# A transformer kernel on one core: output and down projections with the weights moving, layer norms along the free axis

## The chip, the cores and the metric

The kernel runs on one core of a Trainium2 chip. The metric is the device time of one execution in microseconds; three runs of the kernel before took 1226.73, 1228.14 and 1231.18 us, so the median is 1228.14 us. The core has TensorE (PE), which multiplies matrices into PSUM, the vector engine (DVE), the scalar engine (ACT), GpSimd (POOL) and SyncE (SP); here POOL and SP mostly issue DMAs. Work for PE is a product of a stationary operand (128x128, loaded first) and a moving one (128 rows by up to 512 columns).

## What is computed

Two transformer blocks and a third, recurrent one, on 256 tokens of 1024 features, in float32. Only the first two matter here (the recurrent block is left out below):

```python
mod = einsum('bd,ldm->lbm', silu(c), w_mod) + b_mod[:, None, :]
for i in range(2):
    sh_m, sc_m, g_m, sh_f, sc_f, g_f = split(mod[i], 6)
    h = x * (1.0 + sc_m) + sh_m
    y = even_mixer(h, ...) if i == 0 else odd_mixer(h, ...)   # both end with  o @ w_out
    x = layer_norm(ALPHA * x + (1.0 + g_m) * y, ln_mix_g[i], ln_mix_b[i])
    h = x * (1.0 + sc_f) + sh_f
    y = (silu(h @ w_gate[i]) * (h @ w_up[i])) @ w_down[i]
    x = layer_norm(ALPHA * x + (1.0 + g_f) * y, ln_ffn_g[i], ln_ffn_b[i])
```

The layer norm takes mean and variance over the 1024 features of a token. w_out is 1024x1024, w_down 2816x1024.

## The kernel before

**Layout.** Activations lie by feature: tile k of x, h and the rest holds features 128k to 128k+127 on the partitions and the 256 tokens along the free axis (272 with 16 meta tokens in the third block). A float32 product is made of three products in fp32r: every operand is split in a high and a low part, and high x high, high x low and low x high are added in PSUM (`three`, L1815 to L1821).

**Weights.** They stream in units of 128x1024 (`SEGMENTS`, L55: mod, even 20, out0 8, ffn0 44, down0 22, odd 24, out1 8, ffn1 44, down1 22, fqv 24 and on). SP loads two units at a time into `raw` (8 units), ACT makes the high part `whi` (`split`, L551), DVE the low part `wlo` (L982), each with 4 slots, three units ahead of PE (`LEAD`). A slot comes free when PE has done the unit (`units_done`). So unit m+3 is split by ACT and then DVE while PE is at unit m, and every step of `segment` on DVE is such a split and then the stage's own work.

**Stages.** In a wide segment (ffn, odd, fqv) a unit gives one output tile of 128 features: 8 input tiles x 3 products of 256 columns. The first three units of ffn0, odd, ffn1 and fqv run side by side, input tile by input tile, as h comes in (`first_units`). In out0 and out1 (`half`) and down0 and down1 (`deep`) a unit is one input tile with all eight output tiles: 8x3 products of 256 columns, whose stationary operand is a piece of the weights and whose moving operand is the activation. The sums stand in 4 banks of PSUM (two tiles a bank) or in 8.

**The layer norm** (L0 after out0, L1 after down0, L2 after out1, L3 after down1). Since features lie on the partitions, PE makes mean and variance, by products with a matrix of 1/1024:

- DVE: x = y*gate + xa, eight tiles (`residual_half` L1401, `residual_deep` L1355); xa is ALPHA*x, made earlier (`scale_x`, or DVE and ACT in odd);
- PE: eight float32 products of x, the mean (L1908, two passes each); DVE: x - mean (`subtract_mean`, L1036); ACT: squares (L586); PE: eight more, the variance (L1913); five keep-warm products whose result nobody reads (`keep_warm`, L1896); ACT: logarithm and exponential give 1/std (L589, L591);
- DVE, ACT, DVE for each tile: h as float32 (L1063), its high part (L599), its low part (L1068); then PE begins the next segment.

After L3 the RMS norm of the third block follows in the same way, without a mean (`stats(4, T2)`).

**Beside this.** DVE also makes the modulation: `side_sum(n)` (L1009) reduces a side weight of 128x1024 with silu(c), 80 in all; `SIDE_AT` says at which unit of even and out0 the first 22 stand, two more stand in `normalize(0)`, and `ffn0_sums`, the down0 segment and `ffn1_sums` hold the rest. POOL loads the side weights into a ring of five, later four slots (`load_sides`, L2410), and in odd issues the DMAs that turn pairs of q and k (`turn_pair`, L2426).

## Time and profile before

| | |
|---|---|
| median of three runs | 1228.14 us (1226.73 to 1231.18) |
| the profiled execution's own time | 1226.64 us |
| its span, first to last instruction | 1224.9 us |
| busy | PE 1170.8, DVE 883.1, ACT 613.0, POOL 61.8 us |
| granted TensorE clock, mean | 0.988 |
| DMA | 235.41 MB, 192 GB/s |

A profile comes from one execution. An engine's busy time is the time in which at least one instruction of it ran; matmuls overlap in it, since each is shown from its issue until its result is out. PEclk is the clock that was granted to TensorE, 1.00 for 2.4 GHz and 0.50 for 1.2 GHz. A row of the timeline begins with the start and the time in us; in brackets stands how long the engine was idle before it and what ended that.

### The profile page before, as it was taken

To read this page: it belongs to the slowest core of one execution; us is meant where nothing else is said; L and a number is where in the kernel's file an instruction comes from. 1 tells how busy PE (TensorE), PEld (TensorE's weight loads), DVE (VectorE), ACT (ScalarE), POOL (GpSimd) and SP (SyncE) were. 2 spreads that over 40 slices of the span, in tenths; PEclk is the share of its full clock that TensorE was granted. 3 is DMA by queue.
4 is the path that set the end of the run, shared out by engine and by line. 5 is a ranking of instruction groups with operands and counts; after the bars stand their busy time and mean duration, and the time that the engine had idled before them with its cause. 6 is when DMAs were issued, how large, how long until landed. Compare 5 with 4: busy or idle time off the path is not lost.

```text
span 1224.9 us, 24330 instructions
## 1 busy us (share of the span) xinstructions
PE 1170.8 (96%) x9394; PEld 1137.8 (93%) x9394; DVE 883.1 (72%) x1520; ACT 613.0 (50%) x972; POOL 61.8 (5%) x119
## 2 busy tenths in 40 slices
PE   4999989999999999899999999999999999999997
PEld 4898879999998899899999989999999999999997
DVE  5798899988777974686754567877864776877743
ACT  3458545444336665554443365543443645555532
POOL 0100111201102200000000000000000000000000
PEclk9899999999999999999999999999999999999999
DMA  9955658978873643375555514543433453655541
GB/s 352 365 190 192 223 207 320 393 284 306 298 287 96 206 147 138 118 271 195 177 191 181 172 54 153 173 138 104 138 104 104 147 197 109 220 186 173 194 148 35
DMA packets 42430, 235.41 MB, mean 192 GB/s; under 512 B 5872, under 2 KB 8304, under 8 KB 19824
## 3 DMA queue, kind: packets, MB, share of 16 engines
q1 hardware_dynamic: 29808, 190.31, 44.0%
q0 software_dynamic: 12544, 44.05, 10.1%
q8 instruction: 51, 0.84, 0.3%
q14 instruction: 27, 0.22, 0.1%
HBM read 231.19 MB, written 1.05 MB: 190 GB/s over the span
## 4 chain that ended last, share of the span: by engine, by line
PE 82%; DVE 7%; ACT 5%; issue 3%; DMA 1%; SPq 0%; POOL 0%; DVEq 0%; ACTq 0%; POOLq 0%
PE acc L1819 21%; PE acc L1820 21%; PE acc L1821 21%; PE aux L1819 3%; PE aux L1821 3%; PE aux L1820 3%; PE aux L2276 2%; PE aux L1913 2%; ACT whi L551 1%; DVE wlo L982 1%; PE aux L1908 1%; DMA x<-xT 1%; PE aux L1926 1%; DVE lev L1009 1%; PE acc L1896 1%
## 5 line engine op out<-in xcount | busy, mean ns | idle before, releaser
L1819 PE MATMUL acc<-hhi,whi 128*128 128x256 f32 (+3 forms) x1976 | 565.5, 286 | 7.9 <-DVE hlo L1001 3.1
L982 DVE TENSOR_TENSOR wlo<-raw,whi 128x1024 fp32r<-128x1024 f32 x338 | 412.7, 1223 | 209.8 <-ACT whi L551 209.2
L1820 PE MATMUL acc<-hlo,whi 128*128 128x256 f32 (+3 forms) x1976 | 559.6, 283 | 0.0
L1821 PE MATMUL acc<-hhi,wlo 128*128 128x256 f32 (+3 forms) x1976 | 557.1, 282 | 0.0
L551 ACT ACTIVATE whi<-raw 128x1024 fp32r<-128x1024 f32 x338 | 356.6, 1056 | 188.6 <-PE acc L1821 187.3
L1819 PEld LDWEIGHTS acc<-hhi,whi 128*128 128x128 f32 x1976 | 373.4, 189 | 13.6 <-issue 7.4
L1821 PEld LDWEIGHTS acc<-hhi,wlo 128*128 128x128 f32 x1976 | 375.1, 190 | 0.0
L1820 PEld LDWEIGHTS acc<-hlo,whi 128*128 128x128 f32 x1976 | 373.9, 189 | 0.2
L1819 PE MATMUL aux<-ahi,whi 128*128 (+1 forms) x264 | 74.3, 281 | 0.0
L1821 PE MATMUL aux<-ahi,wlo 128*128 (+1 forms) x264 | 74.2, 281 | 0.0
L1820 PE MATMUL aux<-alo,whi 128*128 (+1 forms) x264 | 74.1, 281 | 0.0
L1819 PE MATMUL acc<-ahi,whi 128*128 (+1 forms) x264 | 74.1, 281 | 0.0
L1821 PE MATMUL acc<-ahi,wlo 128*128 (+1 forms) x264 | 74.1, 281 | 0.0
L1820 PE MATMUL acc<-alo,whi 128*128 (+1 forms) x264 | 73.9, 280 | 0.0
L1009 DVE CUSTOM_DVE_ANT_0 lev<-lev,vec 128x1024 f32<-128x1024 f32 x56 | 71.5, 1277 | 0.0
L2410 POOL DMA_DIRECT2D lev<-side_weights x76 | 40.5, 533 | 404.3 <-DVE mods L1009 300.9
L1819 PE MATMUL acc<-mhi,whi 128*128 128x256 f32 (+1 forms) x192 | 56.6, 295 | 3.8 <-DVE mlo L1001 3.8
L1820 PE MATMUL acc<-mlo,whi 128*128 128x256 f32 (+1 forms) x192 | 54.8, 285 | 0.0
L1821 PE MATMUL acc<-mhi,wlo 128*128 128x256 f32 (+1 forms) x192 | 54.6, 284 | 0.0
L728 ACT ACTIVATE side_conv<-acc 128x256 f32<-128x256 f32 x44 | 16.9, 385 | 73.4 <-PE acc L1821 73.4
L1820 PEld LDWEIGHTS acc<-alo,whi 128*128 128x128 f32 x264 | 49.8, 189 | 0.0
L1820 PEld LDWEIGHTS aux<-alo,whi 128*128 128x128 f32 x264 | 49.8, 189 | 0.0
(340 smaller groups left out, 1489.1 us busy)
## 6 DMA issues: line engine op xcount, KB each, us to landing
raw<-weights SPq DMA_DIRECT2D x176, 1024.0 KB, 5.0
lev<-side_weights POOLq DMA_DIRECT2D x76, 512.0 KB, 6.0
big<-side_weights POOLq DMA_DIRECT2D x4, 512.0 KB, 4.7
big<-qkv POOLq DMA_DIRECT2D x32, 64.0 KB, 2.4
x<-xT SPq DMA_DIRECT2D x1, 1024.0 KB, 11.4
raw<-weights SPq DMA_DIRECT2D x2, 512.0 KB, 5.2
out<-x SPq DMA_DIRECT2D x4, 256.0 KB, 2.2
cst<-consts SPq DMA_DIRECT2D x1, 768.0 KB, 8.1
```

Of the source, the lines that this page charges most:

```text
L551: A(whi[:, m % SPLIT, :], raw_unit(i, m), ACT.Copy).then_inc(hi_ready, 1)
L728: A(side[:, k % 2, 0:t], acc[(a0 + j) % 4][:, 0:t], ACT.Silu)\
L982: v.tensor_tensor(wlo[:, m % SPLIT, :], raw_unit(i, m), whi[:, m % SPLIT, :].bitcast(F32), ALU.subtract).then_inc(lo_ready, 1)
L1009: v.tensor_tensor_reduce(part, part, silu_rows[n >= 24], 1.0, V("b_mod", 2 * KT + n), ALU.mult, ALU.add, mods[:, 2 * KT + n:2 * KT + n + 1 ...
L1819: mm(o, whi[:, u % SPLIT, w], hi, start=start, stop=False, skip_group_check=True)
L1820: mm(o, whi[:, u % SPLIT, w], lo, start=False, stop=False, skip_group_check=True)
L1821: return mm(o, wlo[:, u % SPLIT, w], hi, start=False, stop=stop_, skip_group_check=True)
L1896: mm(bank[:, 0:values.shape[1]], C("ones"), values, start=True, stop=True)
L1908: ins = mm(aux[0][:, 0:t], C("mean"), view[:, n, :], start=n == 0, stop=n == KT - 1)
L1913: ins = mm(aux[1][:, 0:t], C("mean"), big[:, 0, n * t:n * t + t], start=n == 0, stop=n == KT - 1)
L2276: ins = mm(o[:, a_:a_ + 64].rearrange("p (n b) -> p n b", b=b), M_[:, h, t0:t0 + P], M_[:, h, t0:t0 + P].rearrange("p (n b) -> p n b", b=2 ...
L2410: pool.dma_start(mod_ring[SIDE_SLOT[n]], side_weights[n]).then_inc(side_loaded[SIDE_SLOT[n]], 16)
```

## The change

- out0, down0, out1 and down1 become "rows" segments (`across`): the activation is the stationary operand, 128 tokens at a time, and the weights move, 512 columns a product. A unit is 4 banks (2 token halves x 2 halves of the 1024 features) x 3 products. In the last unit (out) or the last two (down) the banks come one after the other, so that the first is complete early.
- The sums then lie by token. x, as it goes into the norms, is kept by token too (`tokens`, in the place of xa); it is loaded a second time in that layout. The norm runs along the free axis: DVE multiplies with the gate, adds, and takes bn_stats of four pieces of 512, then bn_aggr; ACT makes 1/std of one column per token half; DVE scales.
- PE transposes the result back, two 128x128 blocks for a tile of h; DVE applies scale and shift from PSUM (`make`), ACT and DVE split it. The transposes of tiles 0 to 3 stand ahead of the next segment, those of 4 to 7 in its first units.
- The mean and variance products are gone; 9 keep-warm products (8 after down) follow the last product.
- Gate, gain and shift must lie along the free axis: POOL writes each gate, divided by ALPHA, to DRAM and reads it back broadcast over the partitions, and loads ln gain and shift likewise, into x's place. `restore` applies gain and shift to `tokens` in the next segment's units 4 to 7 (0 to 3 in odd), in place of `scale_x` and the two passes in odd.
- DVE's last split of a rows segment moves behind the statistics. The modulation sums are placed anew: 24 in even and out0 (one more at unit 6, one more at unit 25), 32 running in ffn0.
- The meta tokens are loaded by POOL in ffn1 rather than by SP at the start.

```diff
-SIDE_AT = [5, 5, 15, 16, 17, 18] + [u for u in range(19, 27) for _ in range(2)]
+SIDE_AT = [5, 5, 6, 15, 16, 17, 18] + [u for u in range(19, 25) for _ in range(2)] + [25, 25, 25, 26, 26]
...
+            def token_norm(L):
+                nc.scalar.preload_act_table_set("natural_log_exp_and_others")
+                for tok in range(2):
+                    act.wait_ge(mv_ready, 2 * L + tok + 1)
+                    st(A(std[:, 28 + tok:29 + tok], std[:, 25 + 2 * tok:26 + 2 * tok], ACT.Ln, bias=LN_EPS / ALPHA ** 2))
+                    st.wait()
+                    A(rstd[:, tok:tok + 1], std[:, 28 + tok:29 + tok], ACT.Exp, scale=-0.5).then_inc(rs_ready, 1)
...
-            norm(1, T1, LN_EPS)
-            h_of_norm(1)
+            token_norm(1)
+            copy_hi(2, T1)
...
+                def gated(b):
...
+                    half = b % 2
+                    st(v.tensor_tensor(scratch[:, 512 * half:512 * half + 512], row_banks[L][b][:, :],
+                                       gate_row(L)[:, 512 * half:512 * half + 512], ALU.mult))
+                def add(b):
+                    half = b % 2
+                    st(v.tensor_tensor(part(b), part(b), scratch[:, 512 * half:512 * half + 512], ALU.add))
+                def spread(b):
+                    st(v.bn_stats(std[:, 6 * b:6 * b + 6], part(b)))
+                def gather(tok):
+                    v.bn_aggr(std[:, 24 + 2 * tok:26 + 2 * tok], std[:, 12 * tok:12 * tok + 12]).then_inc(mv_ready, 1)
+                def scale(tok, a, b):
+                    z = tokens[:, D * tok + a:D * tok + b]
+                    v.tensor_scalar(z, z, std[:, 24 + 2 * tok:25 + 2 * tok], rstd[:, tok:tok + 1], ALU.subtract, ALU.mult)\
+                        .then_inc(u_ready, 1)
...
+                dve.wait_ge(units_done, last + LEAD - SPLIT + 1)
+                split(None, last + LEAD)
+                dve.wait_ge(rs_ready, 2 * L + 1)
+                scale(0, 0, D)
+                dve.wait_ge(rs_ready, 2 * L + 2)
+                scale(1, 0, D // 2)
+                scale(1, D // 2, D)
...
+                def make(n):
+                    dve.wait_ge(tr_mm, 8 * L + n + 1)
+                    v.tensor_scalar(tile[:, n % 4, 0:T1], aux[n % 4][:, 0:T1], affine[:, L, 0, n:n + 1], affine[:, L, 1, n:n + 1],
+                                    ALU.mult, ALU.add).then_inc(h_f32, 1)
+                h_tiles(L + 1, T1, make, 1)
...
             def ffn0_sums(j):
-                if 2 <= j < 26:
-                    side_sum(24 + j - 2)
-                if 26 <= j < 34:
-                    scale_x(1, j - 26)
-                if 31 <= j < 39:
-                    side_sum(48 + j - 31)
+                if 4 <= j < 8:
+                    restore(0, j - 4)
+                if 8 <= j < 40:
+                    side_sum(24 + j - 8)
+                if j == 16:
+                    make_gate(1, 5)
...
+                def part(j, b):
+                    tok, half = divmod(b, 2)
+                    k, m = index(j), m0 + j
+                    t, w = slice(P * tok, P * tok + P), slice(512 * half, 512 * half + 512)
+                    o = banks[b][:, :]
+                    mm(o, high[:, k, t], whi[:, m % SPLIT, w], start=j == 0, stop=False)
+                    mm(o, low[:, k, t], whi[:, m % SPLIT, w], start=False, stop=False)
+                    return mm(o, high[:, k, t], wlo[:, m % SPLIT, w], start=False, stop=j == n - 1)
...
-            wide("ffn0", all_tokens, h_ready, 8, first=3)
-            deep("down0", 0, T1)
-
-            stats(1, T1)
+            wide("ffn0", all_tokens, h_ready, 8, first=3, turned=0)
+            across(1, ahi, alo, lambda j: pe.wait_ge(a_ready, j + 1), lambda j: j, depth=2)
+            keep_warm(8, acc[3], C("past", 256))
...
+            def write_gate(L):
+                pool.wait_ge(gate_ready, L + 1)
+                pool.dma_start(gate_rows[L].rearrange("(k p) -> p k", p=P), gate_column(L),
+                               allow_slow_non_contiguous=True).then_inc(gate_written, 16)
```

How the instructions move is shown at three places. PE from the end of down0 to the start of odd, before:

```order
L1821 MATMUL acc3<-ahi,wlo 128x256
L1908 MATMUL aux0<-x,cst 128x256 [waits y_read] x8
L1913 MATMUL aux1<-big,cst 128x256 [waits sq_ready]
L1913 MATMUL aux1<-big,cst 128x256
...
L1896 MATMUL aux2<-cst 128x256 x5
L1819 MATMUL acc0<-hhi,whi 128x256 [waits lo_ready,acc_free1,acc_free2,h_ready,acc_free0]
```

and after the change:

```order
L1957 MATMUL aux3<-wlo,ahi 128x512
L1932 MATMUL acc3<-cst 128x256 x8
L1940 MATMUL aux0<-cst,xa 128x128 [waits u_ready]
L1940 MATMUL aux0<-cst,xa 128x128
L1940 MATMUL aux1<-cst,xa 128x128 [waits u_ready]
...
L1850 MATMUL acc0<-hhi,whi 128x256 [waits acc_free0,lo_ready,h_ready]
L1851 MATMUL acc0<-hlo,whi 128x256
L1852 MATMUL acc0<-hhi,wlo 128x256
```

The sixteen rows of mean and variance are gone (L1908, L1913), keep-warm products follow the last product at once (L1932), and four pairs of transposes (L1940; xa is the tokens tile, cst the identity) stand ahead of the first product of odd.

DVE at the same place, before:

```order
L982 TENSOR_TENSOR wlo<-raw,whi 128x1024 [waits hi_ready,units_done] x3
L1355 SCALAR_TENSOR_TENSOR x<-aux,mods,xa 128x256 [waits y_ready,side_used,dve_step]
L1355 SCALAR_TENSOR_TENSOR x<-aux,mods,xa 128x256 [waits y_ready] x3
L1355 SCALAR_TENSOR_TENSOR x<-acc,mods,xa 128x256 [waits y_ready] x3
L1355 SCALAR_TENSOR_TENSOR x<-acc,mods,xa 128x256 [waits units_done]
L1036 TENSOR_TENSOR x<-x,aux 128x2x256 [waits mean_ready]
L1036 TENSOR_TENSOR x<-x,aux 128x2x256 x3
L1042 TENSOR_TENSOR affine<-vec,mods 128x8 [waits side_used]
L1043 TENSOR_TENSOR affine<-vec,mods 128x8
L1045 TENSOR_TENSOR affine<-affine,mods 128x8 [waits dve_step]
L1063 SCALAR_TENSOR_TENSOR tile<-x,affine,rstd 128x256 [waits std_ready,affine_ready]
```

and after the change:

```order
L981 TENSOR_TENSOR wlo<-raw,whi 128x1024 [waits hi_ready,units_done] x2
L1060 TENSOR_TENSOR tile<-aux,x 128x512 [waits y_ready,rows_used,gate_loaded]
L1065 TENSOR_TENSOR xa<-xa,tile 128x512 [waits dve_step]
L1060 TENSOR_TENSOR tile<-aux,x 128x512 [waits y_ready]
L1068 BN_STATS std<-xa 128x6 [waits dve_step]
...
L1071 BN_AGGR std<-std 128x2 [waits dve_step]
L1068 BN_STATS std<-xa 128x6 [waits dve_step]
L1071 BN_AGGR std<-std 128x2 [waits dve_step]
L981 TENSOR_TENSOR wlo<-raw,whi 128x1024 [waits hi_ready,units_done]
L1075 TENSOR_SCALAR xa<-xa,std,rstd 128x1024 [waits rs_ready]
L1075 TENSOR_SCALAR xa<-xa,std,rstd 128x512 [waits rs_ready]
```

A gate, an add and a bn_stats for each piece take the place of the residual (L1355) and of the subtraction (L1036); the third split, which stood ahead of the norm (x3), stands behind the second aggregate (L981), and the scaling behind it.

POOL at the start of odd, before:

```order
L2410 DMA lev<-side_weights 128x1024 [waits side_used] x52
L2426 DMA big<-qkv 32x2x256 [waits acc_free1,acc_free0]
L2426 DMA big<-qkv 32x2x256 x3
L2426 DMA big<-qkv 32x2x256 [waits acc_free3,acc_free2]
L2426 DMA big<-qkv 32x2x256 x3
```

and after the change:

```order
L2469 DMA lev<-side_weights 128x1024 [waits side_used] x34
L2474 DMA gate_rows<-affine 128x8x1 [waits gate_ready]
L2495 DMA x<-ln_rows 128x1024 [waits mv_ready]
L2526 DMA big<-qkv 32x2x256 [waits acc_free1,acc_free0]
...
L2526 DMA big<-qkv 32x2x256 x3
L2482 DMA x<-gate_rows 128x1024 [waits rows_used,gate_written]
L2490 DMA x<-ln_rows 128x1024 [waits rows_used]
L2526 DMA big<-qkv 32x2x256 [waits rope_done,acc_free3,acc_free2]
```

The write of a gate and the load of a shift (L2474, L2495) stand behind the side weights, and the reading back of the gate and the load of the next gain (L2482, L2490) between the third and the fourth pair of q and k (L2526).

## Rows read from the trace of the kernel before

**Rows 1.** The page: busy times, and the chain that ended last, by engine.

```profile
PE 1170.8 (96%) x9394; PEld 1137.8 (93%) x9394; DVE 883.1 (72%) x1520; ACT 613.0 (50%) x972; POOL 61.8 (5%) x119
PE 82%; DVE 7%; ACT 5%; issue 3%; DMA 1%; SPq 0%; POOL 0%; DVEq 0%; ACTq 0%; POOLq 0%
```


**Rows 2.** Timeline of PE: start, us, instruction; down0 and the start of odd.

```profile
302.51 0.28 PE L1819 MATMUL aux<-ahi,whi 128*128 128x256 f32 x1
...
364.85 0.28 PE L1821 MATMUL acc<-ahi,wlo 128*128 128x256 f32 x1
...
376.83 0.35 PE L1819 MATMUL acc<-hhi,whi 128*128 128x256 f32 x1 [0.57 <-DVE hlo L1068]
```


**Rows 3.** Timeline of PE after out1 and after down1.

```profile
498.88 0.28 PE L1821 MATMUL acc<-mhi,wlo 128*128 128x256 f32 x1
...
510.59 0.36 PE L1819 MATMUL acc<-hhi,whi 128*128 128x256 f32 x1 [0.57 <-DVE hlo L1068]
...
698.51 0.28 PE L1821 MATMUL acc<-ahi,wlo 128*128 128x256 f32 x1
...
707.60 2.75 PE L1896 MATMUL aux<-cst 128*128 128x256 f32 x12
711.15 4.80 PE L1913 MATMUL aux<-big,cst 128*128 128x272 f32 x16 [0.80 <-ACT big L586]
715.79 2.32 PE L1896 MATMUL aux<-cst 128*128 128x256 f32 x10
718.71 0.36 PE L1819 MATMUL acc<-hhi,whi 128*128 128x272 f32 x1 [0.60 <-DVE hlo L1001]
```


**Rows 4.** Timeline of DVE in the norms after down0 and out1.

```profile
368.98 2.48 DVE L1036 TENSOR_TENSOR x<-x,aux 128x512 f32<-128x512 f32 x4 [1.07 <-PE aux L1908]
...
375.07 0.88 DVE L1063 SCALAR_TENSOR_TENSOR tile<-x,affine,rstd 128x256 f32<-128x256 f32 x2 [3.26 <-ACT rstd L591]
```


**Rows 5.** Timeline of DVE in out0, and of PE at ffn0's start.

```profile
155.02 1.28 DVE L1009 CUSTOM_DVE_ANT_0 lev<-lev,big,vec 128x1024 f32<-128x1024 f32 x1
...
156.23 1.22 DVE L982 TENSOR_TENSOR wlo<-raw,whi 128x1024 fp32r<-128x1024 f32 x1
157.37 1.28 DVE L1009 CUSTOM_DVE_ANT_0 lev<-lev,big,vec 128x1024 f32<-128x1024 f32 x1
...
164.79 0.48 DVE L1401 SCALAR_TENSOR_TENSOR x<-acc,mods,xa 128x256 f32<-128x256 f32 x1
...
176.94 0.36 PE L1819 MATMUL acc<-hhi,whi 128*128 128x256 f32 x1 [0.57 <-DVE hlo L1068]
```


**Rows 6.** Windows: us, busy of PE, PEld, DVE, ACT, POOL, clock, DMA; even, out0.

```profile
80.00:90.00 10.00, 10.00 (x86) 9.50 (x86) 10.00 (x38) 5.20 (x8) 0.00 (x0) 1.00 0.59 206
150.00:165.00 15.00, 14.23 (x107) 12.68 (x105) 13.88 (x22) 7.01 (x9) 3.56 (x7) 1.00 0.90 309
```


**Rows 7.** Timeline of PE in out1, and a group of transposes in odd.

```profile
491.73 0.36 PE L1819 MATMUL acc<-mhi,whi 128*128 128x256 f32 x1 [2.01 <-DVE mlo L1001]
...
447.42 0.60 PE L2187 MATMUL aux<-cst,qkv 128*128 128x128 f32 x4
```


**Rows 8.** Timeline of DVE after down1.

```profile
710.00 0.41 DVE L1083 TENSOR_SCALAR x<-x,vec 128x256 f32<-128x256 f32 x1
```


**Rows 9.** The page's DMA issues: side weights.

```profile
lev<-side_weights POOLq DMA_DIRECT2D x76, 512.0 KB, 6.0
```


**Rows 10.** Windows around the dips of the granted clock.

```profile
489.40:492.80 3.40, 1.39 (x12) 1.21 (x11) 2.71 (x6) 1.76 (x3) 0.53 (x1) 1.00 0.05 19
493.10:496.50 3.40, 3.40 (x19) 3.40 (x18) 0.69 (x1) 0.35 (x1) 1.34 (x3) 0.50 0.79 278
882.20:889.00 6.80, 6.80 (x46) 6.66 (x46) 3.84 (x7) 0.00 (x0) 0.00 (x0) 0.50 0.43 157
25.50:39.10 13.60, 13.23 (x62) 12.94 (x62) 8.18 (x14) 4.72 (x8) 0.00 (x0) 0.50 0.85 305
```

More of the change, by code:

```diff
@@ L1827, in needed, with wide @@
                 return T2 - T3, T2
-            def wide(seg, span, ready=None, before=0, tiles=1, ahead=None, head=1, of=(hhi, hlo), tail=0, first=0):
+            def wide(seg, span, ready=None, before=0, tiles=1, ahead=None, head=1, of=(hhi, hlo), tail=0, first=0, turned=None):
                 _, m0, a0 = START[seg]
@@ L2228, in diff_pieces @@
                     diff_mean(u - 22)
[L2229 removed]
+            wide("odd", all_tokens, h_ready, 16, ahead=diff_pieces, head=24, first=3, turned=1)
             def out1_pieces(r):
```

408 lines of the change are left out of this document (228 added, 180 removed).

## The prediction

> **What bounds the kernel now.** I read the page first, its busy times and its chain [rows 1]. TensorE (PE) is busy 1170.8 of 1224.9 us and has 82% of the chain that ended last. A busy PE is not yet a PE at its peak, so the next view is the price of one product. The timeline of PE in down0 [rows 2] has its first product at 302.51 and its last, the 528th, at 364.85: 62.34 us over 527 steps, 118.3 ns for one product of 256 columns. At the full clock of 2.4 GHz 256 columns take 106.7 ns, so 11.6 ns of each step are not columns. The nearest rows for a long product are the float32 keep-warm products, two passes for 256 columns, so 512 cycles an instruction with its weight load: twelve take 2.75 us and ten 2.32 us [rows 3], 0.215 us for each further one. Only 2 ns of such a step are not cycles.
>
> The second place is the stretch between two stages, where a layer norm holds PE up. After down0 the timeline [rows 2, 4] shows PE on the mean, then the vector engine (DVE) subtracting it, the scalar engine (ACT) squaring, PE on the variance, ACT on logarithm and exponential, DVE and ACT making h, and PE again at 376.83. The last product starts at 364.85 and takes its step of 0.12, so PE is back 11.9 us after its end. After out1 it is 499.00 to 510.59, 11.6 us; after down1, where an RMS norm follows, 698.63 to 718.71, 20.1 us [rows 3]. After out0 PE is back at 176.94 [rows 5]. In all these PE, DVE and ACT take turns, and PE's waits stay under 2 us.
>
> In out0 DVE is the bound beside PE: it is busy 13.88 of 15 us [rows 6], and its rows run without a break of a modulation sum (pitch 1.21 us) and a split (pitch 1.14 us) [rows 5].
>
> **The change part by part.**
>
> *Products.* Out and down of both blocks have (8+22)x2 units of 24 products of 256 columns; now it is 12 of 512. The columns stay the same, so only what is not columns can be saved. Two products of 256 cost 236.6 ns. For one of 512 the ends are 236.6 (the 11.6 ns are a price per column, nothing is saved) and 215 (they hide in a longer product). I take 216, because the row with 512 cycles [rows 3] is the nearer: 20.6 ns saved. Down0 and down1: 2x264x20.6 = **-10.9 us**. Out1: 96x20.6 = 2.0, of which I keep **-1.5**, since PE waits there for the low half of the attention output (2.01 us before 491.73) [rows 7]. Out0: **0** by this, since DVE sets its pace.
>
> The Trainium skill, TensorE: Matmul & The Clock Gate, Back-to-back issue gap, gives for a stream of weight loads and products of N=512 about 131 ns each. By it the 624 products would save 106 ns each instead of 21, and the kernel would fall to some 1168 us. The rows of 512 cycles speak against it with their 215 ns [rows 3].
>
> *The layer norm on DVE.* It now runs on four pieces of 128x512: gate, add and bn_stats for each, then the two aggregates, the affine numbers, the split of the next weight unit (moved behind the norm), and the scaling of 1024, 512 and 512 elements. A tensor_tensor of 128x512 with one operand in PSUM has a pitch of 0.62 us (2.48/4) [rows 4]; I take 0.6 for the gates and the adds. No row shows a bn_stats. Its ends are 0.41 us (a tensor_scalar of 128x256 [rows 8]) and 1.28 us (a sum over 128x1024 [rows 5]); I take 0.6, since it is one more pass over 512 elements. So twelve passes are 7.3 us, one dependent pair adds 0.1, aggregates and affine numbers 0.7, the split 1.15, the scaling until the transposes can start 1.75: 11.1 us from DVE's start (11.0 worked out, 0.1 for the signal), and 0.6 more until DVE is through the last scaling. From the first h piece on DVE to PE it was 375.07 to 376.83 = 1.76 us [rows 2, 4]; I take 1.7. Together **13.3 us from DVE's start to PE's first product**. ACT's part lies beside the split.
>
> When does DVE start? In down the last two units go bank by bank (6 products a bank, 1.3 us), so bank 0 is ready 3.9 us before PE ends. But DVE's last split before the norm waits for ACT, and that for the unit before those two: -5.2 + 1.06 + 1.2, so DVE starts at -2.9. PE is back at +10.4 instead of +11.9: **-1.4** for L1. In out only the last unit goes by banks: bank 0 at -1.95, start at -1.7, PE back at +11.6: **0** for L2. For L0 DVE was through its work at 164.79 [rows 5]. One sum more (+1.21), a split less (-1.14) and 0.6 us of its waits gone put its start at 164.2 and PE back at 177.5 instead of 176.94: **+0.6**. At L3 the transposes start at +7.8 (no affine numbers). Then PE takes turns with DVE and ACT as before, four pairs of tiles being turned, squared and summed; sixteen passes of 272 columns at two cycles each are 3.7 us of it, the turning and the first wait 2.6: 6.3 us. The tail from the last pass to PE's first product, 715.95 to 718.71, stays [rows 3]. PE is back at +16.9 or +17 instead of +20.1: **-3.1**.
>
> *Transposes.* One takes 0.11 us (four in 0.60 with the fill) [rows 7]. Eight of sixteen come before the first product and lie in the wait for h; the other eight stand in the first block, where PE is the bound: 0.9 for each of L0 to L2, **+2.7**.
>
> *A moved sum.* One modulation sum goes from the first norm to unit 6 of even, a stretch in which DVE is busy 10.00 of 10 us [rows 6]: **+1.0**, with 0 and 1.2 as ends.
>
> *Off the path.* ffn0's 32 sums stand in 32 units running: 2x1.14 + 2x1.21 + 0.8 = 5.5 us for two units, and PE needs 5.67, so PE covers them; without that cover each pair would cost the difference. The four restore passes (1.15 us each) take the place of scale_x and of ACT's passes in odd. SP gets a 1 MB load of rows, while its queue runs three units ahead. POOL gets for each norm a write of the gate to DRAM in pieces of 4 bytes, its reading back, and gain and shift, 0.5 MB each; side weights stand behind the wait for each write. Such a load lands after 6.0 us [rows 9] and the ring has four units (11 us) of room. In odd, gate and gain stand ahead of the fourth pair's turning DMAs: 0 to +2; I take 0.
>
> *The clock.* Up to here the sum is -10.9 - 1.5 - 1.4 + 0.6 - 3.1 + 2.7 + 1.0 = **-12.6 us**. But the mean and variance products, which kept PE at work, are gone. After its keep-warm products (18 passes, 3.9 us; 16 at the downs) PE does nothing until the transposes: 5.5 us after out1, 7 after out0, 4.3 to 4.8 after the downs. The windows of the trace show what less has done [rows 10]: PE was busy 1.39 of 3.4 us, and then the granted clock was 0.50 for 3.4 us; other dips last 6.8 and, at the start of the program, 13.6 us. At 0.50 (1.2 GHz) a product takes twice its time, so each us there loses half a us of products. I take the clock as low when the transposes start and as back 5 to 6 us later. The first 2.15 us of that are waits and transposes, so it costs (5.6 - 2.15)/2 = 1.7 us at each of the four norms: **+6.8**.
>
> The Trainium skill says in the same page, Why this matters for your kernels, that idle gaps between bursts of matmuls bring the half clock back. That speaks against this change. The dip at 493.10 [rows 10] agrees, though no row before has a gap of 5 us.
>
> The sum is **-5.8 us** on the profiled execution's 1226.64 (its span is 1224.9): 1220.8. The median of the runs is 1228.14, 1.5 us above it, which gives 1222.3. I predict **1222 us**. About 0.5%, 6.1 us, is what a measurement of this kernel can tell from no change; the forecast lies right at that edge.
>
> **Rivals.**
> - *The clock stays full*, or comes back during the transposes. For it: a gap of this length is in no row. Against it: the dip at 493.10 [rows 10]. It gives -12.6, 1215. Chance 0.17.
> - *Nothing saved in the products*, a price per column. For it: the 11.6 ns on 256 columns [rows 2]. Against it: the 215 ns [rows 3]. It adds 12.4: +6.6, 1234, slower. It decides from 235 ns a product. At 225 ns the gain halves and the time is 1227. Chances 0.05 and 0.08.
> - *The low clock lasts* like the 13.6 us at the start [rows 10]: (13.6 - 2.15)/2 = 5.7 at each of four norms, 23 instead of 6.8: +10, 1238, slower. It decides from 11.5 us of low clock a norm. Chance 0.07.
> - *DVE's chain is longer*: bn_stats at 1.2 us adds 2.4 us a norm, 9.6 in all: +3.8, 1232; slower with a late gate or turning DMA on top. Chance 0.06.
> - *The page's 131 ns*: 1168. Chance 0.01.
>
> **How the numbers follow.** The forecast has the remaining 0.56; a little less than half of it lies beyond -0.5%. Faster: 0.25 of it + 0.17 + 0.01 = 0.43. Same: 0.31 + 0.08 + 0.03 of DVE's chain = 0.42. Slower: 0.05 + 0.07 + 0.03 = 0.15. The range reaches from the full clock, 1214, to the price per column, 1234.
>
> **What would show it.** In down0 264 products 0.216 us apart, and the stage 5.5 us shorter; another pitch sinks the first term. PE back 10.4 us after down0's end and 11.6 after out1's. bn_stats rows of 0.6 us. A granted clock of 0.50 in the first us of ffn0, odd, ffn1 and fqv; 1.00 there would give the faster rival. PE idle in ffn0 for side weights, or DVE waiting for the gate at a norm's start, would mean that POOL's queue matters, and the prediction is wrong.

## The result, and the profile after

The changed kernel takes **1237.14 us** (median of four runs, 1236.27 to 1237.64) against 1228.07 of the kernel before: ratio 1.0069, interval 1.005 to 1.0089. So it is slower by 9 us, where 1222 was forecast and 1234 was the end of the range. The profiled execution took 1237.12 us, its span is 1235.3, and the mean granted clock is 0.972 instead of 0.988.

The page of the changed kernel, lines that answer to [rows 1]: busy times and chain; the clock in 40 slices of the span; then two groups, whose last column is the idle time just before them and what ended it.

```profile
PE 1168.6 (95%) x8636; PEld 1104.7 (89%) x8636; DVE 894.4 (72%) x1502; ACT 596.5 (48%) x954; POOL 71.8 (6%) x134
...
PEclk9899989999998999899999999998999999999999
...
PE 75%; DVE 12%; ACT 5%; issue 4%; DMA 3%; POOL 0%; SPq 0%; DVEq 0%; ACTq 0%; POOLq 0%
...
L1010 DVE CUSTOM_DVE_ANT_0 lev<-lev,vec 128x1024 f32<-128x1024 f32 x56 | 71.5, 1277 | 9.6 <-DMA lev<-side_weights 9.6
...
L1940 PE MATMUL aux<-cst,xa 128*128 128x128 f32 x64 | 14.2, 354 | 17.3 <-DVE xa L1075 17.2
```

PE's busy time fell by only 2.2 us, although 720 pairs of products had become one. DVE's share of the chain went from 7% to 12%, PE waits 17.3 us for the scaled tokens before the transposes (L1940), and DVE waits 9.6 us for side weights, which was to be nothing.

**Where the time went** is read best from when each stage's first product starts, from the timeline of PE (us; the last column is a kernel with repairs that comes below):

| stage | before | changed | difference | repaired (e8) | difference |
|---|---|---|---|---|---|
| out0 | 124.36 | 125.53 | +1.2 | 125.29 | +0.9 |
| ffn0 | 176.94 | 178.63 | +1.7 | 178.68 | +1.7 |
| down0 | 302.51 | 310.16 | +7.7 | 306.02 | +3.5 |
| odd | 376.83 | 381.03 | +4.2 | 376.64 | -0.2 |
| out1 | 464.95 | 471.83 | +6.9 | 466.41 | +1.5 |
| ffn1 | 510.59 | 514.69 | +4.1 | 510.63 | 0.0 |
| down1 | 636.17 | 642.74 | +6.6 | 637.13 | +1.0 |
| fqv | 718.71 | 721.72 | +3.0 | 714.74 | -4.0 |
| end of the span | 1224.9 | 1235.3 | +10.4 | 1220.7 | -4.2 |

Out0 with its norm is 0.5 us longer; the three other projections with their norms are 2.8 to 3.6 us shorter. The wide stage behind each is longer: ffn0 by 6.0, odd by 2.7, ffn1 by 2.5. And 7.4 us appear after fqv's start, in stages that the change doesn't touch. Of out1's 2.8 us, 1.6 are luck of this profile: the kernel before had a stretch of low clock there at 493.10 [rows 10], the changed kernel's first profile has none in out1, and its second (e11), e2, e4, e8 and e10 have it again.

The changed kernel's timeline of PE, which answers to [rows 2, 3]: down0 from first to last product and the start of odd; the end of out1 and the start of ffn1; the end of down1 and the start of fqv.

```profile
310.16 0.40 PE L1955 MATMUL aux<-whi,ahi 128*128 128x512 f32 x1
...
371.19 0.39 PE L1957 MATMUL aux<-wlo,ahi 128*128 128x512 f32 x1
371.42 3.61 PE L1932 MATMUL acc<-cst 128*128 128x256 f32 x16
378.73 1.97 PE L1940 MATMUL aux<-cst,xa 128*128 128x128 f32 x8 [3.69 <-DVE xa L1075]
381.03 0.58 PE L1850 MATMUL acc<-hhi,whi 128*128 128x256 f32 x1 [0.34 <-DVE hlo L1002]
...
503.88 4.05 PE L1932 MATMUL aux<-cst 128*128 128x256 f32 x18
512.38 1.97 PE L1940 MATMUL aux<-cst,xa 128*128 128x128 f32 x8 [4.46 <-DVE xa L1075]
514.69 0.58 PE L1850 MATMUL acc<-hhi,whi 128*128 128x256 f32 x1 [0.34 <-DVE hlo L1002]
...
704.00 3.61 PE L1932 MATMUL acc<-cst 128*128 128x256 f32 x16
711.09 2.27 PE L1940 MATMUL aux<-cst,xa 128*128 128x128 f32 x12 [3.47 <-DVE xa L1075]
...
721.72 0.39 PE L1850 MATMUL acc<-hhi,whi 128*128 128x272 f32 x1 [0.50 <-DVE hlo L1002]
```

Down0 takes 371.42 - 310.16 = 61.26 us for 264 products, **232 ns each**, where two of 256 columns took 236.6 [rows 2] and 216 was forecast. From the last product's end to the next stage's first product it is 9.6 us after down0 (11.9 before), 10.8 after out1 (11.6 before) and 17.7 after down1 (20.1 before). So the norms are shorter, as forecast or more.

DVE's rows in the same norm, which answer to [rows 4]: gate, bn_stats and add, the first aggregate, and the scaling that the transposes wait for.

```profile
368.42 0.68 DVE L1060 TENSOR_TENSOR tile<-aux,x 128x512 f32<-128x512 f32 x1
...
370.35 0.68 DVE L1068 BATCH_NORM_STATS2 std<-xa 128x6 f32<-128x512 f32 x1
370.95 0.67 DVE L1065 TENSOR_TENSOR xa<-xa,tile 128x512 f32<-128x512 f32 x1
...
375.13 0.20 DVE L1071 BATCH_NORM_AGGREGATE std<-std 128x2 f32<-128x12 f32 x1
...
377.40 1.72 DVE L1075 TENSOR_SCALAR xa<-xa,std,rstd 128x1024 f32<-128x1024 f32 x3
```

A bn_stats of 512 elements has a pitch of 0.60 us, like the forecast's.

In ffn0 the delay grows at one place. Timelines of POOL, DVE and PE there:

```profile
230.23 0.91 POOL L2474 DMA_DIRECT2D gate_rows<-affine  x1 [2.22 <-DVE affine L1044]
...
241.58 0.53 POOL L2482 DMA_DIRECT2D x<-gate_rows  x1 [7.87 <-DMA gate_rows<-affine]
...
243.96 1.28 DVE L1010 CUSTOM_DVE_ANT_0 lev<-lev,vec 128x1024 f32<-128x1024 f32 x1 [3.89 <-DMA lev<-side_weights]
...
254.38 1.28 DVE L1010 CUSTOM_DVE_ANT_0 lev<-lev,vec 128x1024 f32<-128x1024 f32 x1 [4.99 <-DMA lev<-side_weights]
...
257.20 0.39 PE L1850 MATMUL acc<-hhi,whi 128*128 128x256 f32 x1 [2.54 <-DVE wlo L981]
```

POOL issues the write of the gate for L1 (1024 numbers of 4 bytes), two side weights, and then stands 7.87 us in front of the read of the gate until that write has landed. The side weights queued behind it come late, DVE waits twice, DVE's split of the weights comes late, and PE stands.

Last, the clock. Windows of the changed kernel over four of the stretches in which it was 0.50 (columns as in [rows 6]):

```profile
378.22:385.05 6.83, 5.99 (x27) 5.59 (x28) 4.78 (x11) 2.09 (x5) 0.00 (x0) 0.50 0.26 101
...
832.20:839.02 6.82, 6.82 (x47) 6.68 (x46) 4.22 (x8) 0.00 (x0) 0.00 (x0) 0.50 0.41 142
852.68:859.50 6.82, 6.82 (x47) 6.68 (x46) 2.51 (x3) 2.02 (x1) 0.00 (x0) 0.50 0.44 153
890.22:900.46 10.24, 10.24 (x62) 9.95 (x62) 4.87 (x7) 0.08 (x1) 0.00 (x0) 0.50 0.30 104
```

There is one at each of the four norms (173.42, 378.22 and 511.34, each 6.8 us, and 712.73, 3.4 us), one behind the wait in ffn0 (258.76), and three in conv, where the kernel before had one [rows 10]. (Conv is a segment of 24 weight units in the third block, behind fqv; between its units stand products of only 64 columns, 32 for each level of pairs.) Half of a stretch is lost where PE has work: up to 3.4, 3.4 and 5.1 us in conv, against 3.4 before.

### The profile page after: what moved, and what is told of

Its sections match the earlier page's. It is cut to its first block, busy times and chain, and to the rows that moved or that the text cites. A ratio compares the mean times of both kernels' runs of the same rounds, so it can differ in the third digit from the quotient of the medians.

```text
span 1235.3 us, 22725 instructions
## 1 busy us (share of the span) xinstructions
PE 1168.6 (95%) x8636; PEld 1104.7 (89%) x8636; DVE 894.4 (72%) x1502; ACT 596.5 (48%) x954; POOL 71.8 (6%) x134
## 4 chain that ended last, share of the span: by engine, by line
PE 75%; DVE 12%; ACT 5%; issue 4%; DMA 3%; POOL 0%; SPq 0%; DVEq 0%; ACTq 0%; POOLq 0%
PE acc L1850 17%; PE acc L1851 17%; PE acc L1852 17%; PE aux L1957 3%; PE aux L1956 3%; PE aux L1955 3%; DVE wlo L981 2%; PE aux L2335 2%; ACT whi L560 2%; DMA lev<-side_weights 1%; DVE lev L1010 1%; DMA x<-xT 1%; PE aux L1852 1%; PE aux L1850 1%; PE aux L1851 1%
## 5 line engine op out<-in xcount | busy, mean ns | idle before, releaser
L981 DVE TENSOR_TENSOR wlo<-raw,whi 128x1024 fp32r<-128x1024 f32 x338 | 412.1, 1221 | 197.7 <-ACT whi L560 197.6
L1957 PE MATMUL aux<-wlo,ahi 128*128 128x512 f32 x176 | 69.5, 395 | 0.0
L1956 PE MATMUL aux<-whi,alo 128*128 128x512 f32 x176 | 69.3, 394 | 0.0
L1955 PE MATMUL aux<-whi,ahi 128*128 128x512 f32 x176 | 69.2, 393 | 0.0
L1956 PEld LDWEIGHTS aux<-whi,alo 128*128 128x128 f32 x176 | 33.1, 188 | 7.8
L1955 PEld LDWEIGHTS aux<-whi,ahi 128*128 128x128 f32 x176 | 33.0, 188 | 7.7
L1957 PEld LDWEIGHTS aux<-wlo,ahi 128*128 128x128 f32 x176 | 33.0, 188 | 7.7
L2335 PE MATMUL aux<-lev 128*128 128x64 f32 x224 | 30.7, 303 | 4.2 <-DVE lev L1577 4.2
L2335 PEld LDWEIGHTS aux<-lev 128*128 128x128 f32 x224 | 30.1, 219 | 4.8 <-DVE lev L1577 4.8
L578 ACT ACTIVATE hhi<-tile 128x256 fp32r<-128x256 f32 (+2 forms) x40 | 16.8, 422 | 30.4 <-DVE tile L1127 26.0
L1955 PE MATMUL acc<-whi,mhi 128*128 128x512 f32 x64 | 27.0, 422 | 4.4 <-DVE mlo L1002 4.4
L1940 PE MATMUL aux<-cst,xa 128*128 128x128 f32 x64 | 14.2, 354 | 17.3 <-DVE xa L1075 17.2
## 6 DMA issues: line engine op xcount, KB each, us to landing
big<-side_weights POOLq DMA_DIRECT2D x4, 512.0 KB, 10.4
```

Source lines behind the costliest of these rows:

```text
L981: v.tensor_tensor(wlo[:, m % SPLIT, :], raw_unit(i, m), whi[:, m % SPLIT, :].bitcast(F32), ALU.subtract).then_inc(lo_ready, 1)
L1955: mm(o, high[:, k, t], whi[:, m % SPLIT, w], start=j == 0, stop=False)
L1956: mm(o, low[:, k, t], whi[:, m % SPLIT, w], start=False, stop=False)
L1957: return mm(o, high[:, k, t], wlo[:, m % SPLIT, w], start=False, stop=j == n - 1)
L2335: ins = mm(o[:, a_:a_ + 64].rearrange("p (n b) -> p n b", b=b), M_[:, h, t0:t0 + P], M_[:, h, t0:t0 + P].rearrange("p (n b) -> p n b", b=2 ...
```

## The experiments

Four questions stood open: what a product costs by its width; what the gate's write costs; what the clock costs at the norms; and whether conv's 7.4 us are of the change at all. Each kernel below was timed together with the kernel before on its chip, and ratios are to that. The kernel before itself ran from 1222.48 to 1233.76 us in 31 runs of one set, so the medians of different sets differ by a us or two.

### e1 and e2: the place in time

A few keep-warm products more in the RMS norm just ahead of fqv (L4 of `stats`) shift what follows.

```diff
 e1, in the kernel before
-                    keep_warm(6 if L == 3 else 5, aux[2], C("past", 256))
+                    keep_warm(6 if L == 3 else 11 if L == 4 else 5, aux[2], C("past", 256))
 e2, in the changed kernel
-                    keep_warm(5, aux[2], C("past", 256))
+                    keep_warm(10 if L == 4 else 5, aux[2], C("past", 256))
```

e1: 

> The kernel before with six more keep-warm products behind the last RMS variance of L3: fqv and all behind it begin about 2.0 us later, nothing else changes. Theory A (the three dips of the granted clock in conv, 7.4 us of the loss, come from the moment at which conv's sparse products run, not from the change): with this shift the old kernel gets dips near 830, 850 and 888 us as the changed one has, and takes 1228 + 2 + 7 = 1237 us. Rival B (something in the changed kernel causes the dips, and a shift costs itself alone): one dip in conv as before, 1230 us.

e2: 

> The changed kernel with five more keep-warm products at the same place, fqv about 1.6 us later. Theory A: conv falls back to the old kernel's alignment, one dip or none in place of three, 1237.1 + 1.6 - 7.4 = 1231 us. Rival B: the three dips stay, 1238.7 us.

e1 took 1226.73 us (ratio 0.9994, 0.9971 to 1.0016), e2 1231.94 (1.0022, 0.9998 to 1.0046). The windows of conv, of the kernel before and then of e1, in which nothing of conv's code differs:

```profile
831.00:836.00 5.00, 5.00 (x50) 4.97 (x47) 2.38 (x6) 1.67 (x2) 0.00 (x0) 1.00 0.56 200
848.00:853.00 5.00, 5.00 (x55) 4.90 (x55) 2.19 (x5) 3.00 (x2) 0.00 (x0) 1.00 0.52 170
```

```profile
831.00:836.00 5.00, 5.00 (x37) 4.86 (x37) 2.94 (x7) 0.00 (x0) 0.00 (x0) 0.50 0.48 154
848.00:853.00 5.00, 4.95 (x30) 4.96 (x31) 4.67 (x4) 1.58 (x2) 0.00 (x0) 0.66 0.31 131
```

50 and 55 products in 5 us at a clock of 1.00, 37 and 30 where it was low. The profiled run of e1 took 1234.59 us with all three stretches. It reached the pairs of level 3 in conv only 0.5 us later than the kernel before: behind a stretch of low clock at the start of the program that was 10.2 us long and not 13.7, its out0 had begun 1.6 us earlier. Seven of its ten runs took 1225.8 to 1228.7 at a mean clock of 0.990 to 0.992. So the same code of conv has one stretch or three, and three cost 7.5 us more than one; that the moment of entry decides it is not shown. Both texts were wrong on the time: e1's median is neither A's 1237 nor B's 1230. e2 came out near A's number (1231), and its profile has one stretch in conv and no further delay there (5.3 us behind the kernel before on entry, 5.3 on leaving).

### e3: the side weights ahead of the gate's read

```diff
-            load_sides(36, 38)
+            load_sides(36, 42)
             read_gate(1)
             load_gain(1)
-            load_sides(38, 72)
+            load_sides(42, 72)
```

> The changed kernel with four more side weights issued ahead of the reading back of the second gate on POOL's queue. Theory (the queue stood 10.4 us behind the write of the gate, and DVE and then PE waited in ffn0 for side weights): ffn0 is 4.3 us shorter and has no dip near 259 us, DVE waits under 1 us for side weights. Rival (the loads compete for DMA bandwidth, and the order is indifferent): ffn0 stays at 131.5 us. What conv does behind it is open, by the theory of alignment up to 7 us either way.

1234.93 us (ratio 1.005, 1.0029 to 1.007). The delay that ffn0 adds behind its first block (its first three units) fell from 4.3 to 1.6 us, and the low clock after it is gone; ffn0 as a whole is 1.9 us shorter, not 4.3. What is left comes later and from another cause. Timeline of DVE and a window of e3:

```profile
264.05 1.28 DVE L1010 CUSTOM_DVE_ANT_0 lev<-lev,vec 128x1024 f32<-128x1024 f32 x1 [3.19 <-DMA lev<-side_weights]
```

```profile
260.00:265.00 5.00, 5.00 (x45) 5.00 (x44) 1.81 (x2) 2.67 (x4) 0.22 (x1) 1.00 1.01 409
```

Now POOL doesn't wait, but the gate's and the gain's broadcast reads, 0.5 MB each, come on top of the weights: the DMA engines are full (share 1.01, 409 GB/s), and a side weight is late. So the term has two parts, the wait in the queue and, by this window, the bandwidth; e9 moves the gain's load and bears on the second.

### e4: longer keep-warm at the norms

```diff
-            keep_warm(9, aux[3], C("past", 256))
+            keep_warm(22, aux[3], C("past", 256))
             wide("ffn0", all_tokens, h_ready, 8, first=3, turned=0)
...
-            keep_warm(8, acc[3], C("past", 256))
+            keep_warm(17, acc[3], C("past", 256))
```

In the same way it is 20 in place of 9 after out1, and 15 in place of 8 after down1.

> The changed kernel with 22, 17, 20 and 15 keep-warm products after out0, down0, out1 and down1 in place of 9, 8, 9 and 8, so that PE works up to the transposes. Theory (the idle stretch lets the clock fall and costs 1.7 us a norm): granted clock 1.00 through all four norms, the first units of ffn0, odd and ffn1 each 1.5 to 2.5 us shorter, fqv begins 5 to 7 us earlier than in the changed kernel. Rival (the clock falls for the transposes too, or the keep-warm products run late): under 2 us in all.

1231.09 us (ratio 1.0018, 0.9996 to 1.0039). No stretch of 0.50 at any of the four norms, and fqv starts as early as in the kernel before (+0.0 instead of +3.0 us). The wait in ffn0 is still there (+4.9 us behind the first block, with its own stretch at 258.45). The text expected 5 to 7 us at fqv against the changed kernel, and 3.0 came. The four norms with the first blocks behind them did gain 6.1 us against the changed kernel's profile; the stretch in out1 (1.5 us), 0.9 us later in odd and 0.6 more of the wait in ffn0 took some 3 of them back. Conv has two stretches here, of 10.2 and 6.8 us.

### e5 and e6: keep-warm in conv, before and after

In conv TensorE waits 1.5, 1.3 and 1.5 us for DVE before the pair products of levels 3, 4 and 6, and those are 32 narrow products each. Levels 3 and 6 in the kernel before:

```profile
826.97 3.79 PE L2276 MATMUL aux<-lev 128*128 128x64 f32 x32 [1.47 <-DVE lev L1546]
...
879.72 4.85 PE L2276 MATMUL aux<-lev 128*128 128x64 f32 x32 [1.47 <-DVE lev L1546]
```

Six keep-warm products go into each wait, into a bank that is free by then:

```diff
                 M_ = level_tiles(n)
+                if n in (3, 4, 6):
+                    pe.wait_ge(pair_read, PAIR_FREE[n, 0])
+                    keep_warm(6, PAIR_BANK[n, 0], C("past", 256))
                 pe.wait_ge(level_ready, n + 1)
```

e5, in the kernel before: 

> The kernel before, with six keep-warm products in front of the waits for level pairs 3, 4 and 6 in conv, where TensorE was idle for 1.47, 1.28 and 1.47 us. Theory A (the low clock in conv comes from this idle time beside the sparse pair products, and falls there in some runs and not in others): no stretch of 0.5 at any of the three places, the runs of this kernel lie closer together than those of the kernel before (1222.5 to 1233.8), and their median is near the lowest of those, 1221 to 1224. Rival B (the pair products alone bring the clock down, the idle time is nothing to it): the stretches stay, the spread too, median 1228. Rival C (the products of this edit delay the pair products, since DVE's chain is what is waited for): 1229 to 1231.

e6, in the changed kernel: 

> The changed kernel with the same six keep-warm products at the same three places of conv. Theory A: the changed kernel's own loss is what it had at the end of fqv, 3.0 us, and the other 7.4 us of its profile were stretches of low clock in conv that have nothing to do with its edit; so this kernel ends 3 to 5 us behind the kernel before with that same edit, near 1226 to 1229, with no stretch of 0.5 between 820 and 900 us. Rival B (the change itself makes conv slower, by what it leaves in buffers or queues): it stays 8 to 10 us behind, 1235 or more.

e5: 1225.12 us (1223.81 to 1227.36 in 12 runs; ratio 0.998, 0.9967 to 0.9992). e6: 1229.99 us (ratio 1.0018, 1.0 to 1.0035). Windows of e6 at the places where the changed kernel had its stretches:

```profile
831.00:836.00 5.00, 5.00 (x56) 4.91 (x55) 5.00 (x9) 0.00 (x0) 0.00 (x0) 1.00 0.00 0
...
885.00:892.00 7.00, 7.00 (x71) 6.83 (x70) 6.01 (x9) 0.00 (x0) 0.00 (x0) 1.00 0.36 108
```

Neither profile has a stretch of 0.50 in conv. e6 starts fqv 3.0 us behind the kernel before and ends its span 2.8 us behind: conv adds nothing any more, and Rival B of e6 is out. From fqv's first product to the end e5 and e6 both take 506.0 us. Against e5, which has the same edit, the change costs 1229.99 - 1225.12 = 4.9 us. Work in the idle time beside the sparse products keeps the stretches away, and Theory A holds in kind; both medians stayed 1 us above its ranges (1221 to 1224, 1226 to 1229). The edit has a price: counted from fqv's start, the pairs of levels 3, 4 and 6 begin 1.0, 2.0 and 2.9 us later in e5 than in the kernel before, and those 2.9 us are about what the one stretch costs the kernel before (506.1 us from fqv to the end). That much of Rival C of e5 is true. e5's runs lie within 3.6 us, where the kernel before spread over 7.6 in the same set; e6's still spread over 8.3.

### e7: the price of a product by its width

```diff
-                    mm(o, high[:, k, t], whi[:, m % SPLIT, w], start=j == 0, stop=False)
-                    mm(o, low[:, k, t], whi[:, m % SPLIT, w], start=False, stop=False)
-                    return mm(o, high[:, k, t], wlo[:, m % SPLIT, w], start=False, stop=j == n - 1)
+                    for of, ws in ((high, whi), (low, whi), (high, wlo)):
+                        for c in range(2):
+                            v = slice(w.start + 256 * c, w.start + 256 * c + 256)
+                            ins = mm(o[:, 256 * c:256 * c + 256], of[:, k, t], ws[:, m % SPLIT, v],
...
-            keep_warm(9, aux[3], C("past", 256))
+            fp32r_row(30, aux[3], mhi, 256, "ffn0")
```

`fp32r_row` issues like products one after the other: 30 of 256 columns after out0, 15 of 512 after down0, 20 of 384 after out1 and 56 of 128 after down1.

> The changed kernel with each product of 512 columns of the output and down projections split into two of 256 into the same bank, the stationary side the same for both; and in place of the keep-warm products, fp32r products of 256, 512, 384 and 128 columns (30, 15, 20 and 56 of them) with the split weights moving, after out0, down0, out1 and down1. Theory A (TensorE's price is per column, about 0.45 ns each, whatever the width): down0 and down1 take as long as in the changed kernel (62.1 and 69.4 us from first to last product, within 1 us), the rows of 15 take 232 ns a product at 512, 175 at 384, 118 at 256, 60 at 128. Rival B (a fixed part per product, which the wide product saves, and which something else in the stage has eaten): the split stages are longer by 4 us or more each, and the 512-column products of the row after down0 take about 216 ns.

1236.4 us (ratio 1.0074, 1.0045 to 1.0103; four runs). Timeline of PE, e7: the first pair of down0, and the four rows of like products.

```profile
310.78 0.40 PE L1958 MATMUL aux<-whi,ahi 128*128 128x256 f32 x2
...
166.36 3.71 PE L1987 MATMUL aux<-whi,mhi 128*128 128x256 f32 x30
...
506.60 3.64 PE L1987 MATMUL aux<-whi,mhi 128*128 128x384 f32 x20
...
373.03 3.66 PE L1987 MATMUL acc<-whi,ahi 128*128 128x512 f32 x15
...
707.81 6.36 PE L1987 MATMUL acc<-whi,ahi 128*128 128x128 f32 x56
```

A group lasts from its first start until its last product is out, so (3.71 - 0.28)/29 = 118 ns for 256 columns, (3.64 - 0.34)/19 = 174 for 384, (3.66 - 0.40)/14 = 233 for 512. That is 0.45 ns a column and less than 5 ns fixed, at and above 256. Down0 took 373.03 - 310.78 = 62.25 us, 1.0 us more than unsplit and 0.2 less than in the kernel before. Theory A holds, with one miss: 128 columns take (6.36 - 0.22)/55 = 112 ns and not 60. Width does save below 256 columns, and this kernel had no such product in its projections. (The 69.4 us for down1 in the text was a slip; down1 has as many units as down0, 61.26 us in the changed kernel.)

### e8: the three repairs together

The edits of e3, e4 and e6 in one kernel.

> The changed kernel with the three repairs together: the six keep-warm products in conv, the side weights 38 to 42 loaded ahead of the second read of the gate, and the keep-warm products after out0, down0, out1 and down1 raised to 22, 17, 20 and 15. Theory A (the change's loss was the sum of a queue wait of 4.3 us in ffn0, four stretches of low clock at the norms, and chance in conv): it is at the start of fqv 3 to 5 us ahead of the kernel before, and ends at 1218 to 1222. Rival B (the repairs don't add, since a delay that one removes is taken up by the next wait in ffn0): 1224 to 1228.

**1220.77 us** (1217.76 to 1222.5, six runs; ratio 0.9944, 0.9925 to 0.9963): faster than both kernels. Windows of e8 over the four norms and conv:

```profile
169.00:181.00 12.00, 11.04 (x63) 9.57 (x62) 11.64 (x26) 2.56 (x9) 0.53 (x1) 1.00 0.38 153
367.00:379.00 12.00, 11.04 (x64) 9.65 (x63) 11.64 (x26) 4.79 (x11) 0.54 (x1) 1.00 0.61 128
500.00:512.00 12.00, 11.04 (x61) 9.67 (x59) 11.71 (x26) 2.22 (x8) 0.53 (x1) 1.00 0.38 143
699.00:716.00 17.00, 15.74 (x80) 12.61 (x80) 13.65 (x29) 8.64 (x18) 2.07 (x3) 1.00 0.05 19
820.00:900.00 80.00, 79.28 (x686) 77.03 (x685) 61.50 (x84) 31.84 (x36) 0.00 (x0) 1.00 0.34 117
```

The clock is 1.00 in all five; the profile has one stretch left between the start and the end of the program, in out1 at 493.82. fqv starts 4.0 us ahead of the kernel before (last column of the table above), so the repairs add up, as Theory A had it. Not all of the gain belongs to the change, since the repair in conv helps the kernel before too: against e5, timed in the same set, e8 is 4.4 us faster (1220.77 to 1225.12, and the slowest run of e8 lies below the fastest of e5).

### e9: three more edits

The sum of even's unit 6 back to the end (three sums in unit 26), the gain's load ten side weights behind the gate's, and nine keep-warm products before out1's last wait.

```diff
-SIDE_AT = [5, 5, 6, 15, 16, 17, 18] + [u for u in range(19, 25) for _ in range(2)] + [25, 25, 25, 26, 26]
+SIDE_AT = [5, 5, 15, 16, 17, 18] + [u for u in range(19, 25) for _ in range(2)] + [25, 25, 25, 26, 26, 26]
...
             read_gate(1)
+            load_sides(42, 52)
             load_gain(1)
-            load_sides(42, 72)
+            load_sides(52, 72)
...
+                if j == 6:
+                    keep_warm(9, aux[3], C("past", 256))
                 pe.wait_ge(o_done, 8 + j + 1)
```

> The kernel with all three repairs, and three more: the side sum of even's unit 6 back behind the others (three in unit 26), the load of the gain ten side weights behind the read of the gate instead of right behind it, and nine keep-warm products ahead of the last wait of out1, where TensorE stood for 2.48 us and the clock fell at 493.8. Theory A (each is a term of its own that stays): even and out0 1.0 us earlier, no step of 0.8 in ffn0, 1.0 to 1.7 us for the clock in out1, in all 1217.5 to 1219.5. Rival B (even waits for something else, and the transfer of the gate alone delays the side weights as much): no more than 1 us, 1220 to 1221.

1221.36 us (ratio 0.994, 0.9918 to 0.9962), not to be told from e8. In its profile out0 begins 2.4 us earlier than e8's. Only 1.2 to 1.8 us of that are the moved sum; the rest is a stretch of low clock at the start of the program that was 10.2 us long here and 13.7 in e8, as it was 10.2 in seven of the thirteen profiles and 13.7 in six. But the third sum of unit 26 stands ahead of the norm on DVE, and PE waits before the transposes in spite of the longer keep-warm:

```profile
174.90 1.09 PE L1940 MATMUL aux<-cst,xa 128*128 128x128 f32 x8 [1.16 <-DVE xa L1075]
```

The clock falls at 177.30, and by the end of ffn0's first block 2.2 of the 2.4 us are given back. The late step in ffn0 (0.8 us) is gone with the gain's load moved, which supports the bandwidth part of e3's account. In out1 the low clock is gone, but out1 is no shorter than e8's (33.3 us from first to last product in e8, 33.4 in e9): the nine products cost what the clock gave. The span is 1.1 us shorter, which the start of the program alone could explain. Neither text fits whole: the terms are there, two of them turned into the next wait.

### e10: the repairs without the longer keep-warm

The edits of e3 and e6 only, so with 9, 8, 9 and 8 keep-warm products at the norms.

> The kernel with the repairs in conv and in POOL's queue, but with the changed kernel's own keep-warm products (9, 8, 9 and 8) at the four norms: it measures the term of the prediction that put the clock at the four norms at 1.7 us each. Theory A (that term is right in size): 5 to 7 us above the kernel with all three repairs, 1226 to 1228. Rival B (most of what the longer keep-warm gave was something else, the clock costs 0.5 to 1 us a norm): 1223 to 1225.

1226.5 us (ratio 0.9983, 0.9966 to 1.0), 5.7 above e8. Windows of e10 over three of the norms:

```profile
169.00:183.00 14.00, 8.10 (x42) 7.25 (x41) 11.24 (x26) 2.90 (x9) 0.53 (x1) 0.76 0.28 107
372.00:384.00 12.00, 7.78 (x42) 7.38 (x42) 8.71 (x22) 3.33 (x10) 0.54 (x1) 0.72 0.35 114
504.00:517.00 13.00, 8.20 (x40) 7.07 (x40) 11.33 (x26) 2.49 (x8) 0.53 (x1) 0.74 0.27 100
```

Theory A holds. The two kernels were timed in different sets; by their ratios to the kernel before they differ by 4.8 us, and e9, timed beside e10, is 5.1 below it. From the start of a projection to the end of the next stage's first block (fqv's start for the last) the four lose 1.4, 2.4, 1.2 and 1.1 us against e8. In e8's windows PE is busy 11 of 12 us in the same places, and the clock stays.

### e11: the changed kernel in more runs

No edit.

> The changed kernel, unaltered, in more runs. What is asked is whether the three stretches of low clock in conv, which its profiled run had and which the kernel with keep-warm products in conv did not, come in all of its runs. Theory A (they come in some runs and not in others, as in the kernel before): runs spread from about 1229 to 1238 in more than one group, median 1232 to 1235. Rival B (in this kernel they always come, since its stages fall just so): all runs within 1235.5 to 1238, median 1237.

1238.74 us (1234.74 to 1240.19; ratio 1.0082, 1.0055 to 1.0109). That is nearer to Rival B, though the runs spread more than its 1235.5 to 1238: with the four runs above, all ten lie above 1234.7 at a mean clock of 0.971 to 0.975, where e6's lay at 0.981 to 0.985. The second profile has its stretches in conv where the first had them:

```profile
833.29:840.12 6.83, 6.83 (x47) 6.69 (x47) 4.44 (x8) 0.00 (x0) 0.00 (x0) 0.50 0.37 127
...
891.32:901.56 10.24, 10.24 (x62) 10.10 (x62) 5.09 (x8) 0.00 (x0) 0.00 (x0) 0.50 0.30 104
```

Against the kernels with keep-warm in conv, by the ratios, its median loses 6 to 8 us, the kernel before 2.5. Which kernel it is does not matter to what the stretches cost, and the moment at which fqv starts does not decide how many come. The profiles without an edit in conv, by that moment:

| profile | fqv starts | stretches of 0.50 in conv | from there to the end |
|---|---|---|---|
| e4 | 718.68 | two (10.2 and 6.8 us) | 510.6 |
| before | 718.71 | one (6.8) | 506.1 |
| e3 | 718.75 | three (6.8, 6.8, 10.2) | 513.6 |
| e1 | 719.07 | three (6.8, 6.8, 10.2) | 513.7 |
| changed | 721.72 | three (6.8, 6.8, 10.2) | 513.6 |
| changed again (e11) | 723.03 | three (6.8, 6.8, 10.2) | 513.6 |
| e2 | 723.88 | one (6.8) | 506.3 |
| e7 | 724.07 | three (6.8 each) | 511.9 |

Three stretches cost the old kernel (e1) as much as the changed one. The profiles in the first three lines start fqv within 0.1 us of each other and have two, one and three. The changed kernel's ten runs show that its loss there comes again and again, and e1's that the kernel before can have it; what decides between one stretch and three is open.

## Why the prediction was wrong

**The products of 512 columns: the step that failed first.** The forecast took 216 ns, "because the row with 512 cycles [rows 3] is the nearer", and -12.4 us from it. Measured: 232 ns, so -1.2 us for each down and 96 x 4.4 ns, -0.4, for out1: **-2.8 in all**. That row was a float32 product in two passes, another kind of instruction. The row of the same kind gave 118.3 for 256 columns, and the bound "a price per column, nothing is saved", which the forecast gave a chance of 0.05, was the right one; e7 shows it at 256, 384 and 512 columns. The float32 row was misread too: a keep-warm product shows as two instructions (`keep_warm(8)` gives x16), each a pass over 256 columns in 215 ns, so it has 0.84 ns for each column it moves, where the fp32r products have 0.45 to 0.46. The Trainium skill's 131 ns (TensorE: Matmul & The Clock Gate, Back-to-back issue gap) is not what these fp32r products do: e7's row has 233.

**POOL's queue: costed at nothing.** The forecast named the wait for the write of the gate, gave it no time, and set 11 us of room against the 6.0 us of a load alone. The DMA issues of the changed kernel give 11.1 us for those 4 KB.

```profile
gate_rows<-affine POOLq DMA_DIRECT2D x4, 4.0 KB, 11.1
```

A queue that waits for that and then for its own loads (6.0 us [rows 9]) is later than a ring of 11 us covers. **+4.3 us** in place of 0 (3.3 to 5.6 in the six profiles without e3's edit); e3 takes 2.7 of it away, and what is left of the step went with the gain's load in e9. The forecast's list of what would show it wrong had this line; its sum didn't.

**The third block: costed at nothing**, and measured at **+7.4 us**. The trace of before already showed it as possible (the stretch at 882.20 in [rows 10] stands at the last of three like places). e5 and e6 settle where it is, and e11 that it comes again with the changed kernel; why it does is open.

**The clock at the norms: right in kind and size.** +6.8 forecast; e10 against e8 gives 4.8 to 5.7, by stages 6.1, and the changed kernel's own profile against e8 5.9. The stretches were 6.8, 6.8, 6.8 and 3.4 us long. PE stood idle for 3.5 to 5.6 us ahead of the transposes. The Trainium skill's rule that idle gaps bring the half clock back (same page, Why this matters for your kernels) agrees with that.

**The norms: right, better than forecast.** PE back 9.6 us after down0 (10.4 forecast), 10.8 after out1 (11.6), 17.7 after down1 in a low clock (17). With the clock full (e8) they are 9.4, 10.7 and 16.3: -2.5, -0.9 and -3.7 against the kernel before, where -1.4, 0 and -3.1 stood. DVE's passes cost what was worked out (0.60 us each); the scaling was quicker, 1.72 us for all 2048 elements. L0 gave back at ffn0's start what was forecast (+0.5 against +0.6).

**Transposes and moved sum: as forecast.** With the clock full (e8) the first blocks of ffn0, odd and ffn1 are each 0.9 us longer, as forecast for the transposes. Behind them ffn0 loses 0.8 to the late side weight, and 0.8 us in odd have no cause shown. Out0 begins 1.2 us later (+1.0 forecast).

The sum on the profiled runs, against the forecast's -5.8: products +9.6, ffn0's queue +4.3, conv +7.4, and the rest 5.1 better. That is +10.4. Of the 5.1, 2.7 are quicker norms, 0.9 the clock at them, and 1.6 the low clock that out1 happened to be without. (In the forecast's working of DVE's chain 11.1, 0.6 and 1.7 add to 13.4 us and not 13.3, which changes nothing here.)

## What to carry to other kernels

- Take a price from rows of the same instruction and data type; if the width changes, fit it per column first. Fewer, wider products save only what lies under the floor of a product, here 112 ns, some 250 columns.
- A change that takes PE out of a wait must bring its own work for PE. Filling the four waits was worth some 5 us here, and filling three in conv, which the change never touched, 2.5 to 8. Look at the granted clock of the whole span, not of the changed stages.
- On a queue the cost of a round trip through DRAM is the wait of everything behind it. Put behind it only what has time.
- Before a loss in an untouched stage is laid to the change or to chance, compare that stage alone in several profiles of both kernels, as the last table does.
